# Expert value rows summed as 64x64 diagonal blocks, two rows to a step of TensorE

## The reference, cut to what matters

```
def block(xb):                              # 128 tokens at a time
    q = (xb @ w_q).reshape(p, 8, 2, 128)    # 8 heads
    s = einsum('phmd,mnd->phmn', q, sub_keys)
    sv, si = top_k(s, 16)
    cand = sv[:, :, 0, :, None] + sv[:, :, 1, None, :]
    best, pos = top_k(cand, 16)             # 16 experts for each token and head
    g = softmax(best)
    act = gelu(einsum('phkd,pd->phk', u_tab[eidx], xb))
    return einsum('phk,phkd->pd', g * act, v_tab[eidx])
```

## Time and profile before

| | |
|---|---|
| median of three runs | 3092.5 us |
| span of the profiled execution, first to last instruction | 3090.2 us |
| its mean granted TensorE clock | 0.969 |
| first row of experts issued to last pass, layer 0 | 774.0 to about 2118 us |
| the same, layer 1 | 2405 to 3075 us |
| data moved by DMA | 926.69 MB, of which 805 MB are the 768 rows |

### The profile page before, as it was taken

How to read it: one execution, slowest core, us unless ns; L and a number is a source line. 1 busy time by engine, 2 the same in 40 slices (tenths; PEclk the granted TensorE clock), 3 DMA queues, 4 the chain that set the end, 5 groups by cost and what they waited for, 6 DMA issues and landing times. The chain is left out here.

```text
span 3090.2 us, 30503 instructions
## 1 busy us (share of the span) xinstructions
PE 2584.4 (84%) x8868; PEld 1266.2 (41%) x8868; DVE 2166.5 (70%) x4962; ACT 637.9 (21%) x1621; POOL 1085.1 (35%) x927
## 2 busy tenths in 40 slices
PE   6997999997899997777777777778988798877777
PEld 2442878774344442222222232223445344432222
DVE  2336555555687788888888888886575777778886
ACT  2134323221211121111111111111024211111111
POOL 0002424312244554444444444451000443444443
PEclk9998999999999999999999999999999899999999
DMA  5243000006799999999999999997422899999998
GB/s 195 77 154 141 1 1 1 1 3 242 285 388 413 408 419 412 418 420 406 420 421 420 421 413 419 420 420 301 169 74 105 346 419 420 420 412 419 420 421 329
DMA packets 137677, 926.69 MB, mean 300 GB/s; under 512 B 17488, under 2 KB 18512, under 8 KB 32104
## 3 DMA queue, kind: packets, MB, share of 16 engines
q0 software_dynamic: 113664, 822.20, 64.9%
q1 hardware_dynamic: 23920, 103.31, 8.8%
HBM read 924.33 MB, written 1.11 MB: 299 GB/s over the span
## 5 line engine op out<-in xcount | busy, mean ns | idle before, releaser
L1605 PE MATMUL psum<-ring,diag 128*128 128x512 f32 x2888 | 1407.6, 623 | 344.5 <-DVE diag L1751 342.5
L1467 POOL DMA_INDIRECT ring<-in_uv,experts x768 | 926.0, 1206 | 1238.2 <-PE psum L1605 937.8
L1807 DVE CUSTOM_DVE_ANT_0 ring<-ring,hcur 128x1024 f32<-128x1024 f32 x768 | 940.6, 1225 | 288.1 <-DMA ring<-in_uv,experts 262.8
L1605 PEld LDWEIGHTS psum<-ring,diag 128*128 128x128 f32 x2888 | 524.5, 194 | 1154.8 <-DVE diag L1751 704.3
L1497 ACT ACTIVATE gel<-dots 128x1 f32<-128x1 f32 x736 | 142.6, 201 | 1384.9 <-DVE dots L1807 1383.8
L1751 DVE TENSOR_SCALAR diag<-ident,gel,wcur 128x128 f32<-128x128 f32 x749 | 252.1, 346 | 26.5 <-ACT gel L1555 19.6
L418 PE MATMUL psum<-zT,win_ring 128*128 128x512 f32 x368 | 160.6, 597 | 5.2 <-PEq L90 5.2
L1877 PE MATMUL psum<-wqkv_ring,zT 128*128 128x512 f32 x320 | 139.3, 598 | 2.9 <-PEq L90 2.9
L1148 DVE COPY_PREDICATED T<-level,psum 128x512 f32<-128x512 uint32 x80 | 57.7, 721 | 99.7 <-PE psum L904 99.7
L1580 PE MATMUL psum<-yT,w_q 128*128 128x512 f32 (+1 forms) x256 | 121.5, 582 | 3.6 <-issue 3.6
L418 PEld LDWEIGHTS psum<-zT,win_ring 128*128 128x128 f32 x368 | 70.0, 192 | 90.7 <-issue 90.7
(11 more groups left out here) (402 smaller groups left out, 2737.5 us busy)
## 6 DMA issues: line engine op xcount, KB each, us to landing
wmod<-in_w_mod SPq DMA_DIRECT2D x32, 1024.0 KB, 8.9
w_q<-in_w_q SPq DMA_DIRECT2D x36, 512.0 KB, 8.0
wmod<-in_w_mod POOLq DMA_DIRECT2D x16, 1024.0 KB, 5.4
ring<-in_uv,experts POOLq DMA_INDIRECT x768, 10.6
wqkv_ring<-in_w_qkv SPq DMA_DIRECT2D x6, 2048.0 KB, 9.2
win_ring<-in_w_in SPq DMA_DIRECT2D x23, 512.0 KB, 3.5
w_all<-in_w_o SPq DMA_DIRECT2D x8, 512.0 KB, 7.3
scores<-in_w_out SPq DMA_DIRECT2D x6, 512.0 KB, 5.8
```

Source lines behind the costliest of these rows:

```text
L1467: nc.gpsimd.indirect_dma_start(ring[:, s % RING], None, uv, bass.IndirectOffsetOnAxis(ap=experts[:, n, j:j + 1], axis=0)).then_inc(row_in[ ...
L1605: m = nc.tensor.matmul(ps[:, c], diag[:, j % DIAGS], ring[:, j % RING, D + 512 * c:D + 512 * c + 512], start=(first and j == 0), stop=(las ...
L1807: nc.vector.tensor_tensor_reduce(u, u, hcur[:], 1.0, 0.0, ALU.mult, ALU.add, dots[:, j:j + 1]).then_inc(dot_done, 1)
```

## The change

Every row goes to TensorE now, and no row is summed by VectorE. The diagonal matrix of a row is kept as two 64x64 diagonal blocks side by side in partitions: `diag` of a row is 128 x 64, made from `eyes`, the sum of the two halves of the identity. A product of a 64x64 block takes 64 partitions in and gives 64 out, one quadrant of TensorE. Two rows are taken in one step (`add_pair`): the even row's blocks are multiplied so that tokens 0 to 63 land in PSUM partitions 0 to 63 and tokens 64 to 127 in 64 to 127; the odd row's cross over. Tokens 0 to 63 use banks 0 and 1, tokens 64 to 127 banks 2 and 3. That is 8 products of 64x64 with 512 columns for two rows, where there were 4 of 128x128.

What follows from it:

- TensorE starts on a pair when its odd row's diagonal is made, and `mm_done` counts up by two at the pair's end: the slot of the even row is released with that of the odd one.
- At a tile's end ScalarE makes four copies of 64 partitions x 1024 (two straight to `sums`, two across to `crossed`) instead of one of 128 x 1024, and `add` has one more addition, `sums` + `crossed` (in the first tile of layer 0 in place of `sums` + `pooled`).
- Queries and scores move to banks 4 to 7, the turns of the last two tiles to 4 and 5.
- TensorE's units are written out instead of looped.

The core of the diff:

```
-        diag = ph.sb("diag", [P, DIAGS, P])
+        diag = ph.sb("diag", [P, DIAGS, HALF])
+        eyes = ph.sb("eyes", [P, HALF])
+        crossed = ph.sb("crossed", [P, D])
...
-                        if RING <= s < HEADS * TOPK + RING and pooled_at((s - RING) // TOPK, (s - RING) % TOPK):
-                            pool.wait_ge(pooled_done, pooled_count((s - RING) // TOPK, (s - RING) % TOPK))
                         if s >= RING:
                             pool.wait_ge(mm_done, DIAGS + s - RING + 1)
...
-                    nc.scalar.activation(sums[:].rearrange("p (c n) -> p c n", c=2), ps[:, 0:2], ACT.Copy).then_inc(out_done, 1)
+                    both = lambda x: x.rearrange("p (c n) -> p c n", c=2)
+                    nc.scalar.activation(both(sums[upper]), ps[upper, 0:2], ACT.Copy)
+                    nc.scalar.activation(both(sums[lower]), ps[lower, 2:4], ACT.Copy)
+                    nc.scalar.activation(both(crossed[upper]), ps[lower, 0:2], ACT.Copy)
+                    nc.scalar.activation(both(crossed[lower]), ps[upper, 2:4], ACT.Copy).then_inc(out_done, 1)
...
+                def add_pair(j0, first, last):
+
+                    for c in range(2):
+                        for j in (j0, j0 + 1):
+                            for r, rows in enumerate((upper, lower)):
+                                m = nc.tensor.matmul(ps[(rows, (lower, upper)[r])[j % 2], 2 * r + c], diag[rows, j % DIAGS],
+                                                     ring[rows, j % RING, D + 512 * c:D + 512 * c + 512],
+                                                     start=(first and j0 == 0), stop=(last and j0 == TOPK - 2), skip_group_check=True)
+                    m.then_inc(mm_done, 2)
+
                 def unit(n, first, last, slot=None, t0=0):
-                    pooled_tile = slot is not None
                     for j in range(TOPK):
                         m, ks = PART_OF(j)
                         if slot is not None and ks:
                             query(slot, m, t0, *ks)
                         if slot is not None and j in SCORE_AT:
                             score(slot, SCORE_AT.index(j), t0)
-                        if pooled_tile and POOLED(j):
-                            continue
-                        take = 2 if pooled_tile and POOLED(j + 1) else 1
-                        pe.wait_ge(diag_done, n * TOPK + j + 1)
-                        for c in range(2):
-                            m = nc.tensor.matmul(ps[:, c], diag[:, j % DIAGS], ring[:, j % RING, D + 512 * c:D + 512 * c + 512],
-                                                 start=(first and j == 0), stop=(last and j + take == TOPK), skip_group_check=True)
-                        m.then_inc(mm_done, take)
+                        if j % 2:
+                            pe.wait_ge(diag_done, n * TOPK + j + 1)
+                            add_pair(j - 1, first, last)
...
-                with pe.Fori(1, HEADS - AHEAD) as hd:
+                for hd in range(1, HEADS - AHEAD):
                     unit(hd, False, False, hd + AHEAD)
...
-                def make_diag(n, j, step, pooled_tile):
-                    if pooled_tile and pooled_at(n, j):
-                        dve.wait_ge(gelu_done, n * TOPK + j + 1)
-                        step(tt(pw[:], gel[:, j:j + 1], wcur[:, j:j + 1], ALU.mult))
-                        nc.vector.scalar_tensor_tensor(pooled[:], ring[:, j % RING, D:], pw[:], pooled[:],
-                                                       ALU.mult, ALU.add).then_inc(pooled_done, 1)
-                        dve.wait_ge(pooled_done, pooled_count(n, j))
-                        return
+                def make_diag(n, j, step):
                     dve.wait_ge(gelu_done, n * TOPK + j + 1)
                     dve.wait_ge(mm_done, n * TOPK + j + 1)
-                    nc.vector.tensor_scalar(diag[:, j % DIAGS], ident[:], gel[:, j:j + 1], wcur[:, j:j + 1],
-                                            ALU.mult, ALU.mult).then_inc(diag_done, 2 if pooled_tile and pooled_at(n, j + 1) else 1)
+                    nc.vector.tensor_scalar(diag[:, j % DIAGS], eyes[:], gel[:, j:j + 1], wcur[:, j:j + 1],
+                                            ALU.mult, ALU.mult).then_inc(diag_done, 1)
...
                     if i == 0:
                         dve.wait_ge(g2_in, 16 * len(SEGS))
-                        if NT == TILES:
-                            tstep(tt(sums[:], sums[:], pooled[:], ALU.add))
+                    tstep(tt(sums[:], sums[:], crossed[:], ALU.add))
```

More of the change, by code:

```diff
@@ L1359, in out_and_experts @@
     PROJ_BANK = lambda i: 4 + 2 * (i % 2)
+    TURN_BANK = lambda i: 2 if i < 2 else 4
+    HALF = P // 2
+    upper, lower = slice(0, HALF), slice(HALF, P)
     LOW = -3.0e38
@@ L1415, in out_and_experts @@
         row_in = ph.sems(*[f"row_in{i}" for i in range(RING)])
-        pooled_done, = ph.sems("pooled_done")
-        POOLED = lambda j: NT == TILES and j % RING == RING - 1
-        FIRST_POOLED = (RING - 1, RING + 1, RING + 3, RING + 5, TOPK - 1) if NT == TILES else ()
-        def pooled_at(n, j):
-            return j in FIRST_POOLED if isinstance(n, int) and n == 0 else POOLED(j)
-        def pooled_count(n, j):
-            if isinstance(n, int) and n == 0:
-                return FIRST_POOLED.index(j) + 1
-            return n * (TOPK // RING) + len(FIRST_POOLED) - TOPK // RING + j // RING + 1
-        if NT == TILES:
-            pooled = ph.sb("pooled", [P, D])
-            pw = ph.sb("pw", [P, 1])
+        eyes_done, crossed_done = ph.sems("eyes_done", "crossed_done")
         with nc.Block() as block:
@@ L1672, in _ @@
                         score(AHEAD, FIRST_SCORE.index(j), 0)
-                    if pooled_at(0, j):
-                        continue
-                    pe.wait_ge(diag_done, j + 1)
-                    for c in range(2):
-                        m = nc.tensor.matmul(ps[:, c], diag[:, j % DIAGS], ring[:, j % RING, D + 512 * c:D + 512 * c + 512],
-                                             start=(j == 0), stop=False, skip_group_check=True)
-                    m.then_inc(mm_done, 2 if pooled_at(0, j + 1) else 1)
-                with pe.Fori(1, HEADS - AHEAD) as hd:
+                    if j % 2:
+                        pe.wait_ge(ev_done, 4)
+                        pe.wait_ge(diag_done, j + 1)
+                        add_pair(j - 1, True, False)
+                for hd in range(1, HEADS - AHEAD):
                     unit(hd, False, False, hd + AHEAD)
@@ L1683, in _ @@
                     unit(hd, False, hd == HEADS - 1, hd + AHEAD, 1)
-                with pe.Fori(1, NT) as t:
+                for t in range(1, NT):
                     pe.wait_ge(out_done, t)
-                    unit(t * HEADS, True, False)
-                    with pe.Fori(1, HEADS - 1) as hd:
-                        unit(t * HEADS + hd, False, False)
-                    unit(t * HEADS + HEADS - 1, False, True)
+                    for hd in range(HEADS):
+                        unit(t * HEADS + hd, hd == 0, hd == HEADS - 1)
             @block.vector
@@ L1758, in _ @@
                 ostep = Chain(dve, out_own)
-                if NT == TILES:
-                    ostep(nc.vector.memset(pooled[:], 0.0))
+                tt(eyes[:], ident[:, upper], ident[:, lower], ALU.add).then_inc(eyes_done, 1)
+                dve.wait_ge(eyes_done, 1)
                 def out(i):
@@ L1809, in unit @@
                         if j >= 2:
-                            make_diag(n, j - 2, step, i == 0)
+                            make_diag(n, j - 2, step)
                         route_part(step, n + 1, j, scored)
-                    make_diag(n, TOPK - 2, step, i == 0)
-                    make_diag(n, TOPK - 1, step, i == 0)
+                    make_diag(n, TOPK - 2, step)
+                    make_diag(n, TOPK - 1, step)
                     dve.wait_ge(diag_done, n * TOPK + TOPK)
```

7 lines of the change are left out of this document (3 added, 4 removed).

## The result

The changed kernel takes 3254.65 us (median of four runs, 3254.38 to 3262.97), the kernel before 3094.1 us beside it (3091.85 to 3097.39): a ratio of 1.052, 95% interval 1.0512 to 1.0536. The forecast was 3102 us with a range up to 3134. The span of the profiled execution is 3253.0 us (3090.2 before), its mean granted clock 0.832 (0.969).

The account below looks back on a forecast made before the run. The prediction took the DMA engines, at 412 to 421 GB/s, as the bound. Its terms, -9 + 7 + 4 + 8 = +10 us on 3092.5, gave 3102.5, forecast as 3102 us, with an 8-in-10 range of 3082 to 3134.

Parts of the forecast that it names:

- The ring of eight in all other units: +7 us: Units outside the first tiles: slots refilled later, 0.25 us a unit lost in 28 units, +7 us, bounds 0 and 36.
- the margin at full clock: Row 4's slot in ordinary units: at full clock nothing is lost, with 0.6 to 1.3 us to spare.
- the lower clock at each pair: Ordinary units: idle TensorE runs every pair at half clock, costing the full 36 us; +39, 3131.5 us; chance 0.14.
- A pair in 2.0 us, 3.7 at half clock: TensorE's sixteen records for two rows: four quadrants at a time, 2.0 us at full clock, 3.7 us at half.
- the rival that they don't: TensorE: quadrants do not run four at a time; about 3150 us at two, some 700 us more at one; chance 0.06.
- First tile of layer 0, -9 us: Units 0 to 7 of layer 0: without VectorE's sums and with shorter TensorE rows, 9 us less; ends 0 and -20.
- The -4 for the stretch in unit 1: Layer 0, unit 1 starts some 3 us sooner; most of 4.0 us lost at 290 GB/s goes, -4 us.
- gaining 5: Layer 0's first tile, units 1 to 7: TensorE and VectorE no longer hold back a slot, -5 of 5.4 us.
- The claim that the query weights lengthen the queue by more than the pair delays: First tiles: query weights in the queue outweigh the pair's delay, so no ring loss was counted there.
- Written-out loops, 0: TensorE's unit loops: the pieces written out move no wait that ends last.
- Ends of tiles, +4: Tile ends: one more addition pass of 1.23 us ahead of a tile's last unit, +4 us; ends 0 and +9.
- The two layer ends, +4 each: End of each layer: four copies instead of one (+3.1) and an addition (+1.23) after the last pairs, +4 us each, +8.

Follow-up runs that it names:

- the kernel released in twos: Kernel before, with GpSimd waiting for the odd row's products before refilling an even row's slot; TensorE still starts each row at once: 3123.7 us, 1.0097.
- the kernel started in twos: Kernel before, with TensorE in later tiles starting two rows at the odd row's diagonal and counting both done at the end, 128x128 products: 3297.7 us, 1.0649.
- the extra products: Changed kernel plus products that only keep TensorE busy in later tiles: two ahead of every row, 3189.0 us; placed after pairs and on even diagonals, 3199.8 us.

## Why the prediction was wrong

**The step that failed is "The ring of eight in all other units: +7 us".** Its mechanism was right, and its full-clock half nearly so: with slots freed in twos at full clock the ordinary units took 40.4 us instead of 40.1. Its size was off by a factor of 16: in place of 7 us the 28 ordinary units cost 111 us more than before (44.1 against 40.1 us each), most of it behind three pairs at half clock. Three things in it were wrong.

- It looked at one slot of eight, that of row 4. The pairs 0-1 and 10-11 lost as much. At full clock they had more time (their slots were issued 5.3 and 6.1 us before the landing of the row ahead in the kernel released in twos, that of the pair 4-5 only 3.9), but at half clock 3.4 and 4.4. Three places instead of one make the bound of the step 28 x 3 x 1.3 = 109 us instead of 36.
- It took the low clock as something that comes often, but not at each pair in full. TensorE waited 7.0, 3.4 and 3.3 us on average ahead of the pairs 0-1, 4-5 and 10-11, and 28, 27 and 26 of 28 of them took over 3 us to the issue: 4.02, 3.83 and 3.74 us on average, against 2.31 at full clock. Ahead of the pairs 6-7 it waited 0.8 us, and 17 of 28 were at full clock. The rows for this were there, and I took 0.25 us a unit from a bound of 1.3.
- It took the shortest landing, 5.5 us, as the limit. That was a row on an empty queue. In the running queue of the changed kernel the loss begins when the issue comes less than 4 to 5 us before the landing of the row ahead, which is 6.5 to 7.5 us before its own. So the margin at full clock was not 0.6 to 1.3 us but about none, as the pairs 4-5 of the kernel released in twos showed.

The step had its evidence in the earlier trace rows: an issue that landed in 6.2 us was on time and the next row 1.3 us late. I read this as a price paid sometimes. It is paid behind each of the three pairs, at 1.1 to 1.4 us on average.

**The rival "the lower clock at each pair"** was nearest to what happened, with a chance of 0.14. Its price, 39 us in all, came from the same one slot; 160 us were measured.

The Trainium skill tells of kernels in which short bursts of products between waits meet the lower clock each time (TensorE: Matmul & The Clock Gate, section HAM oscillation — how this bites in real kernels). The trace agrees: 28 of 28 pairs 0-1 were released 3.7 us or more after their diagonal, and 2.31 us is the figure at full clock.

**A pair in 2.0 us, 3.7 at half clock:** right, 1.95 and 3.69 us for sixteen records. Four quadrants do work at once, and the rival that they don't is out.

The Trainium skill counts 64x64 as four independent tiles (TensorEngine Tiling (Array Packing), section Tiling Modes). The trace agrees for a pair, and shows that one row alone, which uses two of them, gains nothing: 1.93 us.

**First tile of layer 0, -9 us:** the sign was wrong; with the start it is +8.0 us. The -4 for the stretch in unit 1 was about right (unit 1 takes 44.5 us instead of 49.9), but unit 0 took 2.0 us more and units 2 to 7 lost 7.4 instead of gaining 5; the +4.0 at the start differs by as much between kernels that are alike there (777 to 784 us), and nothing is read from it. There TensorE was relieved as expected (196 of 250 us busy, 235 before). That the release in twos took its place is argued, not shown alone: the same +8 us came in units 2 to 7 of the kernel before with that release (265.9 us), and they took 253.1 us with the earlier diagonal; but with each row alone they took 267.3, TensorE then being busy for 237 of 250 us. The claim that the query weights lengthen the queue by more than the pair delays was false, and it also had the first tile of layer 1 at nothing, which cost 13.5 us (302.9 to 316.4; 303.7 with each row alone, 304.7 with the earlier diagonal). VectorE's sums, which the term had as a burden, were worth 11.6 us to the kernel before.

**Written-out loops, 0:** right.

**Ends of tiles, +4:** not separable from the ring. Units 8, 15, 16, 23 and 24 lost 18 us more than before, 3.6 each, no more than the 4.1 of a unit away from the ends.

**The two layer ends, +4 each:** nearly right, and readable in the changed kernel's last unit, beside the earlier trace rows:

```profile
3231.83 6.57 PE L1591 MATMUL psum<-ring,diag 64*64 64x512 f32 x32 [1.82 <-DVE diag L1737]
...
3238.47 1.02 ACT L1503 ACTIVATE sums<-psum 64x1024 f32<-64x1024 f32 x1 [6.69 <-PE psum L1591]
...
3241.56 1.01 ACT L1506 ACTIVATE crossed<-psum 64x1024 f32<-64x1024 f32 x1
3242.61 1.22 DVE L1809 TENSOR_TENSOR sums<-sums,crossed 128x1024 f32<-128x1024 f32 x1 [10.39 <-ACT crossed L1506]
```

Copies +3.1 and addition +1.23 as foreseen; the two last pairs took 6.57 us, not 3.7, where three rows took 5.42. Together +5.5. Of the +10.3 in the table 4.8 are left, about what a unit loses by the ring; they, and the +9.6 of the other layer end, were not taken apart further. The copy's price rested on two points, 379 ns for 256 columns and 1024 ns for 1024, through which a line always runs; the 1.01 to 1.02 us of the copies of 64 partitions bear it out.

One product of the rivals is off and bears on nothing: 8 x 7.1 us a unit for quadrants that don't overlap is some 770 us more, not 700.

## What to carry to other kernels

When work is batched to make an engine faster, write down the round trip of the buffers it frees (here eight rows of 2.49 us, 19.95 us), and go through every slot of it, not one. A speed-up that leaves the engine idle between batches can halve its clock exactly ahead of the batches that are waited for; price those at half clock in full. Where a ring is tight, move its slowest fixed lag first (here the diagonal one row earlier, worth 144 us to the changed kernel and 13 to the old one).

## What was not expected of the hardware

- The DMA queue loses time well before it is seen empty. The time between an issue and the landing of the row ahead (counted as above) does not settle the loss by itself. At 3.5 to 4.0 us it was 1.25 us over two rows in the changed kernel (39 cases, 0.3 to 2.7), 1.20 in the kernel started in twos, 0.85 with the extra products, but 0.23 in the kernel released in twos and 0.29 with half of each pair left out (26 cases each). The sixteen engines ended a row within 1.1 us of each other in the kernel released in twos and within 1.9 us in the changed one (medians). What inside the queue makes the second row late, though it was issued 8.8 us ahead of its landing on average, no run here shows.
- A low clock does no harm in itself: at 0.51 in the stretch, with half the products, the DMA engines moved 414 GB/s.
- A row on two quadrants, eight records in 1.93 us, is as long as on the whole array, 1.98.
